# One head gate tile ahead of the first sums, one down-weight sum ahead of the last strip, context squares one layer earlier

## The reference, cut to what matters

```python
def ffn_sublayer(h, pre_g, post_g, w_up, conv_w, w_down):
    u = rms_norm(h, pre_g)
    z = jnp.einsum("bld,df->blf", u, w_up)
    z = causal_depthwise_conv(z, conv_w)              # 3 taps
    g, up = jnp.split(z, 2, axis=-1)
    y = jnp.einsum("blf,fd->bld", jax.nn.silu(g) * up, w_down)
    return h + rms_norm(y, post_g)
```

```python
s   = einsum(q, k) * exp(dlog - m_t)                  # masked, decayed scores
num = w_inter * einsum(q, C) + einsum(s, v)           # C: the state from the context
den = w_inter * einsum(q, n) + sum(s)
h   = num / max(|den|, exp(-m_t))
out = head_rms(h) * sigmoid(o)
```

## Time and profile before

| | us |
|---|---|
| median of 3 runs | 2090.82 (2089.09 to 2091.09) |
| the profiled execution | 2089.55 |
| its span in the profile | 2087.8 |
| TensorE matmuls busy | 2026.6 (97%) |
| VectorE busy | 1082.3 (52%) |
| ScalarE busy | 565.6 (27%) |
| GpSimd busy | 172.9 (8%) |

### The profile page before, as it was taken

One profiled execution on the slowest core, in us unless ns is written; L12 is line 12 of the kernel. 1 busy time (PEld: TensorE's weight loads), 2 busy tenths in 40 slices (PEclk: granted clock), 3 DMA queues, 4 the chain that ended last, 5 costly groups with the idle time before them and its releaser, 6 DMA issues.

```text
span 2087.8 us, 31438 instructions
## 1 busy us (share of the span) xinstructions
PE 2026.6 (97%) x12813; PEld 1800.3 (86%) x12813; DVE 1082.3 (52%) x2175; ACT 565.6 (27%) x1359; POOL 172.9 (8%) x232
## 2 busy tenths in 40 slices
PE   7999999999989999999999998999999999999998
PEld 5777999877779999888888886788898889989998
DVE  4523997471278875333336335333245445775664
ACT  2343332223433323111110003222323323231212
POOL 5110341011004500000000001000000000000000
PEclk9999999999999999999999999999999999999999
DMA  5353445342545542455554336332322214535452
GB/s 168 106 162 123 162 162 167 117 143 66 164 142 162 185 139 81 142 161 162 162 168 151 111 99 182 100 97 81 93 69 61 82 41 124 178 126 179 162 187 76
DMA packets 274872, 273.61 MB, mean 131 GB/s; under 512 B 11022, under 2 KB 272378, under 8 KB 274730
## 3 DMA queue, kind: packets, MB, share of 16 engines
q1 hardware_dynamic: 273242, 267.77, 40.3%
q0 software_dynamic: 1216, 3.32, 0.6%
q10 hardware_dynamic: 272, 0.52, 0.1%
HBM read 270.38 MB, written 1.08 MB: 130 GB/s over the span
## 4 chain that ended last, share of the span: by engine, by line
PE 88%; DVE 8%; DMA 1%; ACT 1%; issue 1%; SPq 0%; POOL 0%; DVEq 0%; ACTq 0%; POOLq 0%
PE bank L750 44%; PE bank L1183 9%; PE bank L737 8%; PE bank L1352 5%; PE bank L879 3%; PE bank L1366 3%; PE bank L934 2%; DVE arena L2621 2%; PE bank L1417 1%; PE bank L986 1%; PE bank L835 1%; PE bank L1338 1%; DVE arena L2618 1%; PE bank L1379 1%; PE bank L843 1%
## 5 line engine op out<-in xcount | busy, mean ns | idle before, releaser
L750 PE MATMUL bank<-arena,SQ 128*128 128x136 f32 (+2 forms) x2176 | 342.5, 309 | 3.2 <-ACT arena L1713 3.2
L750 PEld LDWEIGHTS bank<-arena,SQ 128*128 128x128 f32 x2176 | 307.7, 191 | 20.6 <-ACT arena L1713 3.6
L750 PE MATMUL bank<-arena,W 128*128 128x136 f32 (+2 forms) x1824 | 273.5, 302 | 3.2 <-issue 3.0
L750 PEld LDWEIGHTS bank<-arena,W 128*128 128x128 f32 x1824 | 248.6, 191 | 14.6 <-issue 3.4
L1713 ACT ACTIVATE H<-bank 128x128 f32<-128x128 f32 (+1 forms) x260 | 82.2, 316 | 509.1 <-PE bank L750 509.0
L750 PE MATMUL bank<-U,W 128*128 128x136 f32 (+2 forms) x1296 | 194.4, 303 | 0.0
L750 PEld LDWEIGHTS bank<-U,W 128*128 128x128 f32 x1296 | 176.5, 191 | 8.5 <-issue 0.4
L737 PE MATMUL bank<-U,W 128*128 128x272 f32 (+2 forms) x608 | 142.2, 395 | 3.9 <-ACT U L1967 2.8
L737 PEld LDWEIGHTS bank<-U,W 128*128 128x128 f32 (+1 forms) x608 | 112.9, 187 | 32.4 <-issue 6.7
L750 PE MATMUL bank<-arena 128*128 128x136 f32 (+1 forms) x1024 | 124.7, 278 | 2.4 <-issue 1.2
L750 PEld LDWEIGHTS bank<-arena 128*128 128x128 f32 x1024 | 120.6, 191 | 3.1 <-issue 1.6
(11 more groups left out here) (408 smaller groups left out, 3011.2 us busy)
## 6 DMA issues: line engine op xcount, KB each, us to landing
W<-in_ffn_w_up_dram SPq DMA_DIRECT2D x44, 1024.0 KB, 5.1
W<-in_ffn_w_in_dram SPq DMA_DIRECT2D x44, 1024.0 KB, 5.1
W<-in_ada_w_dram SPq DMA_DIRECT2D x36, 1024.0 KB, 6.1
W<-in_mix_w_in_dram SPq DMA_DIRECT2D x36, 1024.0 KB, 5.4
W<-in_w_in_dram SPq DMA_DIRECT2D x22, 1024.0 KB, 5.7
W<-in_ffn_w_down_dram SPq DMA_DIRECT2D x16, 1408.0 KB, 6.3
W<-in_ffn_w_out_dram SPq DMA_DIRECT2D x16, 1408.0 KB, 6.3
W<-in_w_out_dram SPq DMA_DIRECT2D x8, 1024.0 KB, 10.3
```

The lines of the kernel that those rows point to most:

```text
L750: last = mm(o, a(k), b[:, k], start=not adds and k == 0, stop=k == kt - 1, skip_group_check=True)
```

## The change

Three edits. In the first mLSTM pair, head gate tile 0 is issued ahead of `sums(0)` (`remember(first=True)`); the other pairs keep their order. In both layers VectorE makes the first weight sum of down strip 0 ahead of the assembly of strip 17 (`first_down_sum`), which makes it wait there for the loads of slots 0 and 1; the four sums are kept in `WDL` in reversed places, so that this one lies clear of buffers still in use. The context squares go from the second to the first layer, and in both layers GpSimd now waits for the products of down strip 1 first.

```diff
@@ -1087,7 +1087,7 @@
 
                 for n in range(4):
                     j = 2 * (n % 2)
-                    down_products(n, T1 // 2, (j, j + 1), lambda i: WDL[:, i], layer_hidden, TDL)
+                    down_products(n, T1 // 2, (j, j + 1), lambda i: WDL[:, 3 - i], layer_hidden, TDL)
                     if l and n == 1:
                         mean_square(SEQ, 5, S.sqc, S.cstat, SQC)
                 output_square()
@@ -1246,7 +1246,7 @@
             def project_values():
                 token_tiles(1, [(2, 0, toks(0)), (2, SW, toks(P)), (3, 0, toks(2 * P)), (3, SW, toks(3 * P))], (2, 3))
 
-            def remember():
+            def remember(first=False):
 
                 eng.wait_ge(S.mqk, p.next(S.mqk))
                 take(4)
@@ -1295,12 +1295,19 @@
                                          [(EE[:, h, 3 * d + b, :], MV[:, s, h, :]) for b, s in blocks])
                     last.then_inc(S.num_full, p.inc(S.num_full))
 
+                def head_gate(t):
+                    if t == 0:
+                        eng.wait_ge(S.land[3], p.next(S.land[3], 16))
+                    take(2 + t)
+                    sem = S.done[3] if t else S.half[3]
+                    group(bank[2 + t][:, 0:SEQ], [(W[3][:, k, t * P:(t + 1) * P], UP[:, k, 0:SEQ]) for k in range(KD)]).then_inc(sem, p.inc(sem))
+
+                if first:
+                    head_gate(0)
                 sums(0)
-                eng.wait_ge(S.land[3], p.next(S.land[3], 16))
-                take(2)
-                group(bank[2][:, 0:SEQ], [(W[3][:, k, 0:P], UP[:, k, 0:SEQ]) for k in range(KD)]).then_inc(S.half[3], p.inc(S.half[3]))
-                take(3)
-                group(bank[3][:, 0:SEQ], [(W[3][:, k, P:2 * P], UP[:, k, 0:SEQ]) for k in range(KD)]).then_inc(S.done[3], p.inc(S.done[3]))
+                if not first:
+                    head_gate(0)
+                head_gate(1)
                 sums(1)
 
             def columns():
@@ -1318,7 +1325,7 @@
             project_values()
             gate_columns()
             for i in range(PAIRS - 1):
-                remember()
+                remember(i == 0)
                 project()
                 columns()
                 project_values()
@@ -1624,8 +1631,9 @@
                     eng.wait_ge(S.order_pool, p.now(S.order_pool))
                     eng.tensor_tensor(WS[n % 2][:, 2], part(0, 0), part(1, 0), ALU.subtract).then_inc(S.first_sums, p.inc(S.first_sums))
                     eng.wait_ge(S.first_sums, p.now(S.first_sums))
-                p.skip(S.prod, 12 + 24)
-                if l:
+                eng.wait_ge(S.prod, p.next(S.prod, 12 + 12))
+                p.skip(S.prod, 12)
+                if l == 0:
                     fill(SQC, 0.0)
                     for k in range(KD):
                         x = H2[:, k, SEQ:2 * SEQ]
@@ -2449,16 +2457,27 @@
                 ins.then_inc(S.tsum, p.inc(S.tsum))
                 eng.wait_ge(S.tsum, p.now(S.tsum))
 
-            def down_sums(n, slots, o, hidden=None, sums=None):
+            def first_down_sum(slots, o):
+
+                for r in slots:
+                    eng.wait_ge(S.land[r], p.next(S.land[r], 16))
+                x, y = (W[r][:, :, P:2 * P] for r in slots)
+                tt(o(0), x, y, ALU.add).then_inc(S.wsum, p.inc(S.wsum))
+                eng.wait_ge(S.wsum, p.now(S.wsum))
+
+            def down_sums(n, slots, o, hidden=None, sums=None, begun=False):
 
                 a = lambda t, h: W[slots[h]][:, :, t * P:(t + 1) * P]
                 steps = ((0, a(1, 0), a(1, 1), ALU.add), (1, o(0), a(0, 0), ALU.subtract),
                          (3, a(0, 1), o(1), ALU.subtract), (2, a(0, 0), a(1, 0), ALU.subtract))
-                for r in slots:
-                    eng.wait_ge(S.land[r], p.next(S.land[r], 16))
+                if not begun:
+                    for r in slots:
+                        eng.wait_ge(S.land[r], p.next(S.land[r], 16))
                 for i, (to, x, y, op) in enumerate(steps):
                     if n == 0 and i < 3:
                         down_token_sums(hidden, sums, i)
+                    if begun and i == 0:
+                        continue
                     tt(o(to), x, y, op).then_inc(S.wsum, p.inc(S.wsum))
                     eng.wait_ge(S.wsum, p.now(S.wsum))
                 if n == 0:
@@ -2608,6 +2627,10 @@
 
                     for s in range(2):
                         n = 2 * (g - 2) + s
+                        if n == 17:
+                            for r in range(SLOTS):
+                                p.skip(S.land[r], 16 * (4 if r > 1 else 5))
+                            first_down_sum((0, 1), lambda i: WDL[:, 3 - i])
                         assemble(s, T1 // 2, SNL[:, s], lambda t: Z[:, g % 2, 2 * s + t, :], (S.zt, S.zt), ((2 + n) % 4,))
                         for t in range(2):
                             i = 2 * s + t
@@ -2642,11 +2665,9 @@
                 p.count.update(counted)
                 for g in range(2, 11):
                     up_products(g)
-                for r in range(SLOTS):
-                    p.skip(S.land[r], 16 * (4 if r > 1 else 5))
                 for n in range(4):
                     j = 2 * (n % 2)
-                    down_sums(n, (j, j + 1), lambda i: WDL[:, i], layer_hidden, TDL)
+                    down_sums(n, (j, j + 1), lambda i: WDL[:, 3 - i], layer_hidden, TDL, n == 0)
                     if l and n == 1:
                         context()
                     for m in range(2 * n - 2, 2 * n):
```

## The result

| | before | changed |
|---|---|---|
| median | 2090.82 us (2089.09 to 2095.27, 9 runs) | 2078.80 us (2077.10 to 2086.93, 9 runs) |
| the profiled execution | 2089.55 us | 2078.25 us |

The ratio of the changed kernel to the one before is 0.9946, with a 95% interval of 0.9937 to 0.9956: faster by 0.54%, about 11 to 12 us (the interval is 9.2 to 13.2 us). The number predicted was 2077.5.

A forecast was written before the change was run, and what follows sets the result against it. TensorE, busy 97%, bounds the kernel, so only its stands and slow clock count. Terms 1.75 + 1.75 + 1.74 + 7.5 = 12.75 us off 2089.55 give 2076.8, or 2078.1 on the median's footing; forecast 2077.5, range 2072 to 2083.

The forecast's parts named there:

- What bounds the kernel: Whole kernel: TensorE's matmul row is busy 97% of the span, so only what makes it stand or run slower counts.
- First layer, 1.75 us: Down strip 0, first layer: early weight sum fits VectorE's idle 1.62 us, so product 6 starts 1.75 us earlier.
- Second layer, 1.75 + 1.74 us: Down strip 0, second layer: 1.75 us from the same early sum, 1.74 us from the squares leaving strips 16 and 17.
- the contention term: Second layer: squares beside VectorE's strips 16 and 17 cost TensorE 1.74 us, from 23.95 against 22.21 us in the first.
- The squares' new place, 0: First layer, behind down strip 1: squares last about 14.2 us, VectorE's weight sums still come in time; cost 0.
- the factor 1.7: Down strip 2, first layer: VectorE slowed beside the squares by 0.85/0.50, so a weight sum takes 2.8 us.
- First mLSTM pair, 7.5 us: Tile 0 ahead of `sums(0)`: `sums(1)` starts 7.5 us earlier, 3.25 of stand and 4.26 of clock.
- rival (a): First pair: the clock falls all the same, only the stand is won; 8.5 us gained, 2081 us; chance 0.1.
- The room of 0.3 us: First pair: tile 0 runs until 1309.39 and the decay tile is ready at 1309.1, leaving 0.3 us.
- The sum: Whole kernel: 1.75 + 1.75 + 1.74 + 7.5 = 12.75 us less, forecast given as 2077.5 us.
- rival (b): Other stands of about 3 us change their clock: 2072.5 with three low stretches lost, 2081 with two gained; chance 0.15.
- the prediction's own signs of being wrong: `sums(0)` waiting over 1 us, VectorE's idle before strip 17's assembly becoming a load wait, or untouched stands changing their clock.

The follow-up runs named there:

- Run 3: Kernel before with only the context squares moved to the first layer, behind down strip 1; 2089.62 us, ratio 0.9991 to the kernel before.
- Run 2: Kernel before with only the early down-weight sum in both layers, squares left in the second layer; 2089.83 us, ratio 0.9998 to the kernel before.
- Run 5: Full change with the fill and the context squares made twice; 2078.11 us, ratio 0.9943 to the kernel before.
- run 6: Full change, but only four of the eight matmuls of head gate tile 0 ahead of `sums(0)`; 2080.99 us, ratio 0.9952 to the kernel before.
- run 4: Full change without GpSimd's new wait, so the squares run beside strips 16 and 17 of the first layer; 2083.12 us, ratio 0.9962 to the kernel before.
- run 8: Full change, with tile 0 and four of the eight matmuls of tile 1 ahead of `sums(0)`; 2080.35 us, ratio 0.9949 to the kernel before.
- run 9: Full change, but both head gate tiles of the first pair ahead of `sums(0)`; 2085.39 us, ratio 0.9972 to the kernel before.
- run 7: Full change, but six of the eight matmuls of head gate tile 0 ahead of `sums(0)`; 2079.43 us, ratio 0.9947 to the kernel before.

## Why the prediction was right, step by step

**What bounds the kernel.** Right: the gain is the stands removed and one low-clock stretch, to within 0.1 us at each place, and VectorE and GpSimd, slower where they meet, cost nothing. (A slip in the prediction and in rows 6: the row pairs at 327.73 and 724.74 are the first product of strip 17, not 16; the stretches compared are the same in both kernels, so no number hangs on it.)

**First layer, 1.75 us.** Right in kind, 1.65 measured. The sum fits the idle time (331.12 to 332.74, assembly at 332.78), no stand is left for a down sum, and product 6 comes at 20.56 us, where 20.4 to 20.5 was forecast. Of the lost tenth, 0.07 us is in the first product behind the stand, which takes 2.62 us and not 2.55, and the rest in products 3 and 4, 5.15 us instead of 5.10. The rows showed the first already, 2.79 against 2.71 us for a group that follows a stand, and I had taken 2.55 throughout.

**Second layer, 1.75 + 1.74 us.** 3.49 forecast, 3.40 measured, the same tenth. Run 3 gives the contention term by itself, 1.74. The prediction had it only as a difference of the layers. The rows show its two halves: 0.93 us less stand for the hidden tile (1.97 to 1.04), and 0.81 us from strip 17's first product to down product 1 (7.29 to 6.48), where TensorE had stood 0.54 us for a ScalarE snapshot. Run 2 shows the condition that the prediction wrote down, that VectorE's idle time must return there: without it the early sum costs 1.63 us, nearly all of it the low clock, instead of gaining 1.75.

**The squares' new place, 0.** Right, with both numbers behind it off. I used the factor 1.7 of a short VectorE instruction and expected 2.8 us for a sum; it takes 1.92 to 2.04, so 0.3 to 0.4 us more. The factor was the wrong form: the loss is a piece of time for each instruction, 0.35 us on 0.50 and 0.3 to 0.4 us on 1.62. GpSimd's own time was forecast unchanged at 14.2 us and is 17.5, because it is the one that waits, up to 2.00 us for an add of 0.72. The Trainium skill ("SBUF — State Buffer", "Who interferes with whom") says that the port pair which the two engines share is an exclusive lock. The trace agrees: 1.62 us sums of VectorE make GpSimd late by up to 1.28 us, and GpSimd's adds of 0.72 us cost VectorE 0.3 to 0.4. Run 5 doubles the load and still finds nothing.

**First mLSTM pair, 7.5 us.** 7.58 measured: 3.25 of stand and the rest clock. `sums(1)` starts 1312.74 - 1301.95 = 10.79 us behind the end of the open gate, against 10.7 forecast. The size rests on one execution of the kernel before: in runs 2 and 3, whose pair is as before, the stands are 3.07 and 3.45 us and the open gate to `sums(1)` takes 21.69 and 21.03 us instead of 21.93. The tile stands at 1301.95, inside the 1300 to 1304 named. The clock rows say 1.00 for the whole of 1300 to 1312, so rival (a) did not happen. The Trainium skill's rule ("TensorE: Matmul & The Clock Gate", "What's actually happening"), that activity lifts the half rate, stood in the prediction for the case that sparse matmuls might not hold it up. It did not come about here: with no stand ahead of them, the 64-row sums ran here at full pace, as in the third pair. Behind a stand the clock was low over these sums: 8.3 us at 0.59 with four of eight matmuls ahead, 9.7 us at 0.50 with both tiles.

The room of 0.3 us that I gave the decay tile is 0.23 in the profiled execution, and there the prediction was too sure: it took one execution's chain as fixed, and run 6 shows the same chain 1.5 us later. In an execution where it comes that late, the full change would stand about 1.3 us. A smaller case is on record: run 4 has the pair as in the full change, and its rows came 3.04 us behind the start of the open gate instead of 2.38.

```profile
1311.13 3.86 PE L1183 MATMUL bank<-arena 64*128 64x129 f32 x20 [0.41 <-DVE arena L2938]
```

There `sums(0)` stood 0.41 us, and the clock stayed at 1.00. In the eleven profiles the rows come 2.01 to 3.86 us behind that start, in nine of them by 2.78; how often the full change stands in its other executions is open.

**The sum.** 12.75 forecast, 12.63 measured at the places of the change, and 11.30 between the two profiled executions. The difference is rival (b), which had 0.15: stands that the change doesn't touch changed their clock. The prediction gave 2081 for two such low stretches gained; what happened is a smaller form of it, 0.86 and 0.67 us at two stands, less 0.26 at the start. Stands that change their clock were also among the prediction's own signs of being wrong. That sign came, and it was worth 1.53 us; it leaves the three places of the change as they were forecast. The forecast of 2077.5 is 0.75 us under the profiled execution and 1.3 us under the median; single executions move by more than that, since the nine runs of the changed kernel spread over 9.8 us. So that the number came out within 1.3 us is in part luck; the terms at the places of the change are not.

Whether the change causes those two low stretches, or they fall as they may, is not settled. Three things speak for chance. The single executions spread by more than the effect. In runs 2 and 4 the same stand of 3.6 us was followed by the low level once and not the other time. And run 5, which has all three edits, loses nothing in either stretch against the kernel before: from down product 6 of the first layer to strip 17 of the second it takes 374.39 us, where the kernel before takes 374.80 and the changed one 375.66, and from down product 6 of the second layer to the open gate 553.34 us against 553.48 and 554.15. But no run changed the clock behind a stand by itself.

## What to carry to other kernels

Price an edit by the stretch between two landmarks that stand in both orders, and compare a twin of the stretch (another layer, another pair) where the suspected cost is absent: 22.21 against 23.95 gave the contention term without a run. Ask of each filler where its room comes from: the early sum was worth nothing in the second layer until another engine's work had left, and a pair of edits must then be judged as a pair. A clock loss that one profile shows behind a stand is not a fixed price: look for a second profile of the same place. To cover a stand with work from behind it, move no more than covers it, for what is moved was itself covering the next wait; and where it costs nothing, give the landing of a small transfer a microsecond or two of room beyond what one profile shows (run 8 had that room and paid 1.26 us elsewhere for it).

## What the runs showed of the hardware that was not expected

- A stand of TensorE can cost more than its length: behind stands of 2.96 us (run 6), 2.98 us (run 9, both tiles) and 3.64 us (run 2) the granted clock was 0.59, 0.50 and 0.61 in the stretch that follows. Yet behind 3.63 us in run 4 it was 1.00, with the same matmuls following as in run 2, and around the stands of 0.79 us (run 7) and 1.26 us (run 8) it was 1.00 for all of 1305 to 1325.
- The low level may begin within a stand: at the end of the first layer the changed kernel stands from 409.25 to 412.30, and its clock is 0.50 in 411 to 412. The kernel before stands as long, from 411.16 to 414.21, and its clock is 1.00 throughout.
- GpSimd's adds of 0.72 us took up to 2.00 us beside VectorE's 1.62 us sums, while these grew only to 1.92 to 2.04. The engine that lost most was the one with the shorter instructions.
- The read-back of a few rows from DRAM took 4.47 us in one execution and 5.71 in another, with the same program on its queue. What else the DMA engines carried at that moment was not separated.
